# Decay mixer: 64x64 products on all four quadrants of TensorE, chunks 1 to 3 on swapped partition halves, levels placed by predicated copies

## The reference, cut to what matters

```python
def step(S, xt):
    r_t, w_t, k_t, v_t, a_t, b_t = xt
    sa = jnp.einsum('bhij,bhj->bhi', S, a_t)
    S = S * w_t[:, :, None, :] + sa[..., :, None] * b_t[..., None, :] + v_t[..., :, None] * k_t[..., None, :]
    return S, jnp.einsum('bhij,bhj->bhi', S, r_t)
_, ys = lax.scan(step, jnp.zeros((B, H, N, N), F32), xs)
```

## Time and profile before

| | |
|---|---|
| median of three runs | 2735.07 us |
| profiled execution, its own time | 2733.12 us |
| its span, first to last instruction | 2731.2 us |
| TensorE busy | 2675.1 us, 98% |
| VectorE busy | 1812.3 us, 66% |
| ScalarE busy | 1413.5 us, 52% |
| chunk products, levels and scan | 1326.3 to 1439.9 us of the span |

### The profile page before, as it was taken

One profiled execution on the slowest core, in us unless ns is written; L12 is line 12 of the kernel. 1 busy time (PEld: TensorE's weight loads), 2 busy tenths in 40 slices (PEclk: granted clock), 3 DMA queues, 4 the chain that ended last, 5 costly groups with the idle time before them and its releaser, 6 DMA issues.

```text
span 2731.2 us, 47800 instructions
## 1 busy us (share of the span) xinstructions
PE 2675.1 (98%) x19686; PEld 2413.6 (88%) x19686; DVE 1812.3 (66%) x2213; ACT 1413.5 (52%) x1872; POOL 141.8 (5%) x227
## 2 busy tenths in 40 slices
PE   7999999999999999999999999999999999999999
PEld 7899999888998888879998888889988888899887
DVE  5555688766566666679757667666566676656665
ACT  5544577655555455458325445454345454455544
POOL 3000000100000000000301000000000000000000
PEclk9989999999999999999999999999999999999999
DMA  7165799665535555544304556556445555553553
GB/s 210 47 209 173 260 358 357 231 201 194 154 131 193 193 185 193 185 138 139 111 4 142 196 186 202 185 170 198 150 170 193 187 191 188 196 153 130 196 186 123
DMA packets 371308, 491.97 MB, mean 180 GB/s; under 512 B 12320, under 2 KB 331392, under 8 KB 371136
## 3 DMA queue, kind: packets, MB, share of 16 engines
q1 hardware_dynamic: 367984, 479.51, 53.1%
q0 software_dynamic: 2576, 7.97, 1.0%
q10 hardware_dynamic: 576, 1.98, 0.2%
HBM read 488.38 MB, written 1.05 MB: 179 GB/s over the span
## 4 chain that ended last, share of the span: by engine, by line
PE 93%; DVE 3%; ACT 2%; issue 1%; POOL 1%; DMA 0%; ACTq 0%; DVEq 0%; POOLq 0%
PE bank L367 21%; PE bank L366 11%; PE bank L346 9%; PE bank L348 9%; PE bank L347 9%; PE acc L346 8%; PE acc L348 8%; PE acc L347 8%; PE bank L3152 1%; PE bank L3129 1%; PE bank L3140 1%; DVE w_lo L316 1%; PE bank L1679 0%; PE acc L711 0%; DVE X L579 0%
## 5 line engine op out<-in xcount | busy, mean ns | idle before, releaser
L316 DVE TENSOR_TENSOR w_lo<-raw,w_hi 128x2048 fp32r<-128x2048 f32 x349 | 798.7, 2291 | 411.7 <-ACT w_hi L311 411.3
L311 ACT ACTIVATE w_hi<-raw 128x2048 fp32r<-128x2048 f32 x349 | 667.0, 1913 | 256.8 <-PE acc L348 222.5
L367 PE MATMUL bank<-act_both,w_hi 128*128 128x512 f32 x2560 | 654.8, 392 | 1.5 <-DVE w_lo L316 1.5
L367 PEld LDWEIGHTS bank<-act_both,w_hi 128*128 128x128 f32 x2560 | 465.2, 189 | 84.8 <-DVE w_lo L316 1.9
L366 PEld LDWEIGHTS bank<-act_both,w_lo 128*128 128x128 f32 x2560 | 349.2, 190 | 25.0
L346 PE MATMUL acc<-w_hi,mix_hi 128*128 128x512 f32 x920 | 361.5, 393 | 4.0 <-ACT att_probs L1350 2.2
L348 PE MATMUL acc<-w_hi,mix_lo 128*128 128x512 f32 x920 | 359.1, 390 | 0.0
L347 PE MATMUL acc<-w_lo,mix_hi 128*128 128x512 f32 x920 | 358.6, 390 | 0.0
L366 PE MATMUL bank<-act_both,w_lo 128*128 128x256 f32 x2560 | 357.0, 282 | 0.0
L904 ACT ACTIVATE scratch<-bank 128x256 f32<-128x256 f32 x320 | 121.7, 383 | 426.8 <-PE bank L367 420.3
L346 PE MATMUL bank<-act_both,w_hi 128*128 128x256 f32 x1032 | 296.3, 287 | 6.0 <-DVE act_both L3455 2.6
(11 more groups left out here) (557 smaller groups left out, 3977.2 us busy)
## 6 DMA issues: line engine op xcount, KB each, us to landing
raw<-in_ffn_w_gu SPq DMA_DIRECT2D x176, 1024.0 KB, 5.1
raw<-in_ffn_w_down SPq DMA_DIRECT2D x88, 1024.0 KB, 4.9
raw<-in_ml_w_in SPq DMA_DIRECT2D x24, 1024.0 KB, 5.3
raw<-in_rt_w_in SPq DMA_DIRECT2D x24, 1024.0 KB, 5.2
raw<-in_w_up SPq DMA_DIRECT2D x20, 1024.0 KB, 8.0
raw<-in_w_gate SPq DMA_DIRECT2D x19, 1024.0 KB, 7.5
raw<-in_w_down SPq DMA_DIRECT2D x18, 1024.0 KB, 7.1
moe_raw<-in_w_down SPq DMA_DIRECT2D x14, 1024.0 KB, 7.1
```

Source lines behind the costliest of these rows:

```text
L311: act.activation(w_hi[0:rows, slot, 0:size], raw[0:rows, slot, 0:size], ACT.Copy).then_inc(hi_made, 1)
L316: dve.tensor_tensor(w_lo[0:rows, slot, 0:size], raw[0:rows, slot, 0:size], w_hi[0:rows, slot, 0:size].bitcast(F32), ALU.subtract).then_inc ...
L367: return pe.matmul(bank[b][:, :], w_hi[:, slot, w], act_both[:, k, :], start=k == 0, stop=k == KT - 1)
```

## The change

A product is given a source half and a destination half. With `dst` 1 the result of head 2k is written to partitions 64 to 127 and that of head 2k+1 to 0 to 63; those matmuls use the two quadrants off the diagonal. `beside` issues a product on the diagonal and one off it, taking turns after each pair of heads; `alone` issues one by itself. ak, rk, V2 and K2 of all chunks are kept swapped, and of chunks 1 to 3 (`RW_SWAP`) also Z and the inverse. So that the inverse can be swapped and X's other factor not, chunks 1 to 3 have one more product, Ti, the same as T but swapped. VectorE no longer adds the identity or Y and X: ScalarE fills `rw_inv` and `rw_Y` with the identity (`"fill"`, two instructions of 128x2048) once `tilde` is done, and VectorE copies each result over it where the level's mask is set (`copy_predicated`; at the chunk products for Ti, BT and chunk 0's T, at the levels for every Y and X). The matrix of all levels is masked once, with `strict`, into `rw_L` (lying in `rw_tmp` and `rw_S`), so the masking of each level is gone. Z goes to `acc` banks 0, 1, 2, 0 and X of chunk 3 to `acc3`. In the scan, the right-hand side's part from ak of the next chunk is issued beside the y part from rk. TensorE gets a counter `rw_pe` of its own, on which it waits before it adds to a result that it began from other partitions. The table of constants, loaded at the start, is 256 columns wider.

```diff
-        RW_EV += [(x, c) for c in range(CHUNKS) for x in ("T", "BT", "ak", "rb", "rk", "V2", "K2", "B2")]
-        for l in range(1, 6):
-            RW_EV += [("Z", ch, l) for ch in range(CHUNKS)]
-            RW_EV += [(x, ch, l) for ch in range(CHUNKS) for x in "YX" if x == "Y" or l < 5]
+        RW_EV += [(x, 0) for x in ("T", "ak", "BT", "rk", "rb", "V2", "B2", "K2")]
+        RW_EV += [(x, c) for c in range(1, CHUNKS) for x in ("T", "Ti", "BT", "ak", "rb", "rk", "B2", "V2", "K2")]
+        for l in range(1, 5):
+            RW_EV += [("Z", 0, l), ("Z", 1, l)] + [("Y", 3, l - 1)] * (l > 1) + [("Z", 2, l), ("X", 0, l), ("Z", 3, l)]
+            RW_EV += [("Y", 0, l), ("X", 1, l), ("Y", 1, l), ("X", 2, l), ("Y", 2, l), ("X", 3, l)]
+        RW_EV += [("Z", 0, 5), ("Z", 1, 5), ("Y", 3, 4), ("Z", 2, 5), ("Y", 0, 5), ("Z", 3, 5)] + [("Y", ch, 5) for ch in (1, 2, 3)]
...
+        Z_BANK = [0, 1, 2, 0]
+        RW_SWAP = [0, 1, 1, 1]
+        rw_L = [rw_tmp[:, 0, :], rw_tmp[:, 1, :], rw_S[:, 0, :], rw_S[:, 1, :]]
...
+            def one(k, b, left, right, src, dst):
+
+                for par in range(2):
+                    rows = rows_of[par ^ src]
+                    last = pe.matmul(b[rows_of[par ^ dst], k * L:k * L + L], left(rows, k), right(rows, k), start=True, stop=True)
+                return last
...
+            def beside(first, second):
+
+                for k in range(8):
+                    last, other = one(k, *first), one(k, *second)
+                done(last)
+                done(other)
...
+            for first, second in (("T", "ak"), ("BT", "rk"), ("rb", "V2"), ("B2", "K2")):
+                beside(chunk_product(first, 0), chunk_product(second, 0))
+            for ch in range(1, CHUNKS):
+                for first, second in (("T", "Ti"), ("BT", "ak"), ("rb", "rk"), ("B2", "V2")):
+                    beside(chunk_product(first, ch), chunk_product(second, ch))
+                alone(chunk_product("K2", ch))
+
+            def z(ch, l):
+                if l == 1:
+                    rw_dve.wait(pe, ("base", ch))
+                elif ch < 3:
+                    wait_evacuated(pe, N["X", ch, l - 1])
+                else:
+                    rw_dve.wait(pe, ("X", 3, l - 1))
+                if ch == 3:
+                    rw_act.wait(pe, ("Z", 0, l))
+                return acc[Z_BANK[ch]], small(rw_L[ch]), local(rw_Y, ch), 0, RW_SWAP[ch]
+
+            def grown(x, ch, l):
+                rw_act.wait(pe, ("Z", ch, l))
+                if l > 1:
+                    wait_evacuated(pe, N["Y", ch, l - 1])
...
+            for l in range(1, 6):
+                beside(z(0, l), z(1, l))
+                if l == 1:
+                    alone(z(2, l))
+                else:
+                    beside(grown("Y", 3, l - 1), z(2, l))
+                if l == 5:
+                    beside(grown("Y", 0, l), z(3, l))
+                    for ch in range(1, CHUNKS):
+                        alone(grown("Y", ch, l))
+                else:
+                    beside(grown("X", 0, l), z(3, l))
+                    beside(grown("Y", 0, l), grown("X", 1, l))
+                    beside(grown("Y", 1, l), grown("X", 2, l))
+                    beside(grown("Y", 2, l), grown("X", 3, l))
...
                 for half in range(2):
                     b = B("u", ch, half)
+                    wait_evacuated(pe, N["Y", ch, 5])
                     rw_act.wait(pe, ("rhs", ch, half))
...
+                    if ch < 3:
+                        wait_evacuated(pe, N["V2", ch + 1])
+                        last, other = both_parts(y_product, (half, acc[half], local(rw_ak, ch + 1), chunk_of(rw_v, ch + 1),
+                                                             1, RW_SWAP[ch + 1], True, False))
...
-                if ch < 3:
-                    for half in range(2):
-                        rw_act.wait(pe, ("rhs", ch, half))
-                        parts(half, acc[half], local(rw_ak, ch + 1), chunk_of(rw_v, ch + 1), True, False)
...
+            rw_dve.wait(act, "tilde")
+            diagonal = C("ident2").unsqueeze(1).to_broadcast([P, 8 * CHUNKS, L])
+            act.activation(rw_inv[:, :, :].rearrange("p c (k s) -> p (c k) s", s=L), diagonal, ACT.Copy)
+            rw_act.done(act.activation(rw_Y[:, :, :].rearrange("p c (k s) -> p (c k) s", s=L), diagonal, ACT.Copy), "fill")
             rw_dve.wait(act, "bonus")
...
+            def where(dst, name, b):
+
+                return dve.copy_predicated(eight(dst), mask(name).bitcast(I32), eight(b))
...
+            rw_act.wait(dve, "fill")
             for ch in range(CHUNKS):
...
+                for x in ("ak", "BT", "rk", "rb") if ch == 0 else ("Ti", "BT", "ak", "rb", "rk"):
+                    b = got(x, ch)[:, :]
+                    if x == "Ti":
+                        last = where(rw_inv[:, ch, :], "level0", b)
...
+                if ch == 0:
+                    where(rw_inv[:, ch, :], "level0", acc[ch][:, :])
+                rw_dve.done(dve.tensor_tensor(eight(rw_L[ch]), eight(acc[ch][:, :]), mask("strict"), ALU.mult), ("base", ch))
                 if ch == 0:
                     ahead(16)
...
+            for l in range(1, 5):
+                placed("X", 0, l)
+                placed("Y", 0, l)
+                for x in "XY":
+                    for ch in range(1, CHUNKS):
+                        placed(x, ch, l)
+            for ch in range(CHUNKS):
+                placed("Y", ch, 5)
```

More of the change, by code:

```diff
@@ L2990, in block_kernel @@
         rw_dve = Steps("rw_dve", RW_DVE)
-        RW_ACT = [("m", j) for j in range(4)] + ["e+", "end", "e-"]
+        RW_ACT = [("m", j) for j in range(4)] + ["e+", "end", "e-", "fill"] + [("Z", ch, l) for l in range(1, 6) for ch in range(CHUNKS)]
         for ch in range(CHUNKS):
@@ L2995, in block_kernel @@
         rw_act = Steps("rw_act", RW_ACT)
+        RW_PE = []
+        for ch in range(CHUNKS):
+            RW_PE += [("kv", ch, 0), ("kv", ch, 1)] * (ch < 3)
+            for half in range(2):
+                RW_PE += [("rkv", ch, half)] + [("akv", ch + 1, half)] * (ch < 3)
+        rw_pe = Steps("rw_pe", RW_PE)
         rw_pool = Steps("rw_pool", ["ka", "norm", "bonus"] + [("rstd", *p) for ch in range(CHUNKS) for p in RW_PARTS[ch]])
@@ L3122, in pe_rw @@
             rw_dve.wait(pe, "tilde")
[L3123 to L3160, removed]
+            rows_of = [slice(0, 64), slice(64, 128)]
             def local(a, ch):
@@ L3169, in small, with square_ident, alone @@
                 return lambda rows, k: a[rows, k * L:k * L + L]
+            def square_ident(rows, k):
+                return ident[rows, rows]
+            def one(k, b, left, right, src, dst):
[3 more added lines that the diff above has]
+                return last
+            def alone(first):
+                for k in range(8):
+                    last = one(k, *first)
+                done(last)
@@ new lines, in beside, with chunk_product @@
+            def beside(first, second):
+                for k in range(8):
+                    last, other = one(k, *first), one(k, *second)
+                done(last)
+                done(other)
+            def chunk_product(x, ch):
+                left, right = {"T": (rw_a, rw_h), "Ti": (rw_a, rw_h), "BT": (rw_h, rw_a), "ak": (rw_k, rw_h), "rb": (rw_a, rw_r),
+                               "rk": (rw_k, rw_r), "V2": (rw_v, None), "K2": (rw_k, None), "B2": (rw_a, None)}[x]
+                return (acc[ch] if x == "T" else B(x, ch), chunk_of(left, ch),
+                        square_ident if right is None else chunk_of(right, ch), 0, int(x in ("Ti", "ak", "rk", "V2", "K2")))
@@ new lines, in part, with parts @@
+            def part(k, half, b, left, right, src, dst, start, stop):
+                at = slice(k * L, k * L + L)
+                for par in range(2):
+                    rows = rows_of[par ^ src]
+                    last = pe.matmul(b[rows_of[par ^ dst], at], left(rows, 4 * half + k), right(rows, 4 * half + k),
+                                     start=start and k == 0, stop=stop and k == 3)
+                return last
+            def parts(*product):
+                for k in range(4):
+                    last = part(k, *product)
+                return last
@@ L3171, in state, with both_parts @@
+            def both_parts(first, second):
+                for k in range(4):
+                    last, other = part(k, *first), part(k, *second)
+                return last, other
             def state(ch):
```

98 lines of the change are left out of this document (47 added, 51 removed).

## The result

The change brings nothing; if anything the kernel is slower by 0.13%. The kernel after takes 2740.03 us (median of 20 runs, 2736.19 to 2743.02), the kernel before 2734.86 beside it (20 runs, 2730.14 to 2741.2): ratio 1.0013, 95% interval [1.0007, 1.0019], which is 3.6 us more by the ratio and 5.2 by the medians. The prediction, 2703, is wrong by 37 us, and 2740 lies outside its range. The profiled execution of after took 2738.49 us (before 2733.12), and its span is 5.5 us longer.

The account below looks back on a forecast made before the run. TensorE, busy for 98% of the span, was taken as the bound. Before the scan 30.5 us won, scan 1.9, constants -0.2: 32.2 us less than the median 2735.07, so 2703; range 2697 to 2730, the forecast's own 2697 to 2710.

Parts of the forecast that it names:

- the price of a slot: Chunk products and levels: a slot, one `beside` pair or one product `alone`, taken at 0.933 us; 49 slots for 91 products.
- the upper bound: Chunk products and levels: 1.87 us for a slot of two products, if only two quadrants ever run together.
- Rival 1: 64x64 products: TensorE fed no faster than one record per 29.2 ns, or quadrants take turns; 2737 us, chance 0.11.
- Rival 2: 64x64 products: steady rate between 29.2 and 14.6 ns, a pair 1.40 us at the middle; 2719 us, chance 0.09.
- The rule weighed against the change: 64x64 products: an issue floor of about 25 ns per matmul makes a pair 1.6 us, the kernel some 2726.
- Ti: Chunk products: one new product in each of chunks 1 to 3, making 8 + 3 x 9 = 35, in 19 slots.
- The waits of the chunk products: TensorE waiting for VectorE: 1.8 us for the fill, 2.0 behind `ahead(16)`, 2.2 for turns of the banks.
- The predicated copies: Levels, VectorE: eight a level at 0.60 us each, 4.8 us, under TensorE's 5.6; upper bound some 1.2 us each.
- Rival 3: Levels: predicated copies at 1.2 us make VectorE the bound, 9.6 us a level; 2721 us, chance 0.09.
- The scan: Next chunk's ak product beside the rk product: 1.9 us won for chunks 1 and 2, nothing for chunk 3.
- theory A: From the experiments, not the prediction: the supply of TensorE instructions, about 256 per 3.75 us, sets the pace.
- The constants: Load at the start, 256 columns (128 KB) wider: 0 to 1.6 us of cost, 0.2 taken.

Follow-up runs that it names:

- experiment 3: Kernel before plus five stretches of 512 matmuls each, on two or four quadrants with 64, 128 or 8 columns: 2912.82 us in its one run.
- experiment 2: Kernel after without the three Ti products, 192 TensorE instructions fewer, the layer's result being another: 2737.52 us, ratio 1.0004 to before.
- experiment 1: Kernel after with the two products of every pair issued one after the other instead of taking turns: 2739.72 us, ratio 1.0012 to before.
- experiment 5: Kernel after with chunk products that share a left operand made in one 128-column matmul, 1728 instructions for 2240: 2732.76 us, ratio 0.9993 to before.
- experiment 6: Kernel after with shared-left-operand products merged and Ti replaced by two 64-partition predicated copies, 1536 chunk-product instructions: 2734.08 us, ratio 1.0004 to before.
- experiment 7: Kernel after with merged products, no Ti, and T's placing moved behind the banks' release, read from SBUF: 2730.87 us, ratio 0.9985 to before.
- experiment 4: Kernel after with operands of the 64x64 products read as bfloat16 upper halves, half the instructions, coarser result: 2694.41 us, ratio 0.9853 to before.

## Why the prediction was wrong

**The step that failed is the price of a slot.** "Lower bound: 0.933 us, if each quadrant keeps its 58 ns ... I take 0.933." Each quadrant does keep its 58 ns, and inside a block a pair of products does take 0.93 us: 256 instructions in 1.88 us before the stop at 1382.7, one matmul record per 14.6 ns. But two pairs are a block, and a block comes every 3.8 us; a pair costs 1.9 us on the average, the upper bound, which the prediction gave to quadrants that can't run together. The prediction read 29.2 ns from record to record as a property of the array (58 ns a quadrant, two quadrants). That was true and a coincidence: the supply of instructions allowed 29 ns as well, and a full TensorE row can't show a second limit that stands at the same place. The instruction queue was a row of the page and was not read; 23 packets in the stage, at 256 instructions each, would have shown a period of 3.7 us beside the 3.73 us of four products. Neither of the two ways in which the prediction said that it could be wrong came true: four quadrants do run together, and VectorE hands the banks back in time for most of the stretch.

**Rival 1** had the time (2737) and half the mechanism: "TensorE is fed at one record per 29.2 ns and no faster". Chance 0.11 was too little. Of its two readings the feeding is right, the quadrants' turns are wrong (experiment 3). **Rival 2**, a steady rate between 29.2 and 14.6 ns, was wrong in kind: the rate is 14.6 within a block and 29 to 30 over whole ones.

**The rule weighed against the change.** The issue floor of about 25 ns from one matmul to the next (the Trainium skill, TensorE: Matmul & The Clock Gate, Back-to-back issue gap) would have made 2726. The trace doesn't agree with it: float32 records on four quadrants start every 14.6 ns within a block. The page that does bear on the case is Runtime: NRT & Kernel Launch, Instruction fetch mechanics, of the same skill: instructions come in blocks of 16 KiB, 256 of them. The trace agrees, with a packet of 16 KB per 3.7 us. The page also calls the cost of a block's boundary "mostly hidden"; that holds for the kernel before (TensorE busy in 51.78 of 52 us) and not for after, with a stop in every block.

**Ti** was counted with a slot more in each of three chunks, 2.8 us. It costs that, as 192 instructions: experiment 2 gave 2.5 by the medians.

**The waits of the chunk products** came in part as walked: TensorE stopped for the fill at 1327.7 for 1.6 us (forecast 1328.1, 1.8 us), but behind `ahead(16)`, 2.33 us of the chain, for only 0.8 (forecast 2.0), by these waits from 1326 to 1412 us:

```profile
PE bank L3152 <- DVE rwm_ak L3662: 2.0, 2, 1.5
...
PE bank L3152 <- DVE rw_w L3642: 0.8, 1, 0.8
```

They hardly show in the total: the stage's 32.8 us are its instructions at 14.6 ns, where the levels, nearly without such waits, need 15.2. That the supply goes on meanwhile is the likely reason; no run isolates it. The granted clock averaged 0.94 over that stage; the prediction had left it at full.

**The predicated copies** were taken at 0.60 us from start to start. Rival 3 is out: by its group (busy us, mean ns) one takes 0.72 us, and by VectorE's order of time two in a row take 1.32, so 0.6 from start to start:

```profile
L3642 DVE COPY_PREDICATED rw_xx<-con,bank 128x512 f32<-128x512 int32 x16 | 11.1, 720 | 9.0 <-PE bank L3152 8.6 <-PE acc L3152 0.4
```

```profile
1370.23 1.32 DVE L3642 COPY_PREDICATED rw_w<-con,bank 128x512 f32<-128x512 int32 x2
```

**The scan** was to win 1.9 us and lost 1.9 (53.6 to 55.5). Its number of instructions is the same in both kernels, so that nothing can be won is clear by theory A. Where the loss comes from no run here isolates: it stayed at 55.2 to 56.6 in experiments 1, 5, 6 and 7 and was 53.7 in experiment 2, which doesn't touch the scan, so it may be where the stops fall; that stays open. With half the instructions, in experiment 4, it took 50.2 us (1372.0 to 1422.2). **The constants** (968 KB in 10.6 us where 840 took 10.7) cost nothing that can be seen here.

**Two small sums** of the prediction don't come out as written: 17.7 + 1.8 + 2.0 + 2.2 is 23.7 and not 23.6, and five levels at 0.28 us are 1.4 and not 1.2. Neither matters beside the slot.

## What to carry to other kernels

TensorE has two budgets, array time and instructions, and only the first is in its busy row. Count the instructions of a stage (a float32 matmul is four here: two matmul records, each with its weight load) and put 3.5 to 3.8 us for each 256 of them beside the busy time; if the two are close, splitting the array further is worth nothing, and a longer instruction, a shared left operand or a single pass (one record for a matmul) is. The 3.5 to 3.8 us are from this kernel alone. After a change that lowers an engine's busy time and not the span, compare the counts of records in the same stretch: an unchanged count says at once that the pace is set elsewhere.

## What was new about the hardware

- TensorE's instructions arrive in packets of 16 KB on a DMA queue of their own. In streams of short instructions one comes every 3.4 to 4.5 us, only one is under way at a time, and TensorE stands still between its last instruction and the next block. The fastest stretch needed 3.45 us a block, for the most part at a granted clock of 0.50; whether blocks can come faster was not tried.
- Four 64x64 quadrants take float32 matmuls of 128 columns at twice the rate of two (28.2 against 56.5 us for 512 matmuls), also where the diagonal and the other pair write to the same partitions in different banks, and changing between them for each pair of heads costs nothing that can be seen: 256 instructions with 32 changes took 1.88 us, where two slots without a change are 1.87.
- In after's levels, with a stop in every block, the granted clock stayed at 1.00; in experiment 4, with one-pass bfloat16 records, half as many of them, it was 0.50 in the same stage.
